# Recurrent-branch projection units computed with tokens in partitions, scaled by ScalarE, turned by VectorE in 32x32 blocks; convolution taps placed later

## The chip, the cores and the metric

The kernel runs on 1 core of one Trainium2 chip. The metric is the device time of one launch in microseconds (us). Weights come from HBM; activations, split weights and intermediate slabs stay in SBUF, and matmul sums are built in PSUM.

## The reference, cut to what matters

Two transformer-like blocks are computed in float32 for 256 tokens of width 2048. The change touches the first part of the first one:

```
h    = rmsnorm(x, norm_mix_pre)
proj = h @ w_in                       # columns: xr 2048, yr 2048, q 2048, k 256, v 256, gates 4096
xr   = causal_depthwise_conv(xr, conv_w, conv_b)    # y[t] = b + sum_k x[t-3+k] * w[k], 4 taps
xr   = rg_lru(xr, ...)                # gates by small matmuls, then a scan over tokens
y_rnn = xr * gelu(yr)
q, k = rope(q), rope(k)
y_att = sliding_window_sink_attention(q, k, v, attn_sinks)
mix  = sigmoid(g_rnn) * (y_rnn @ w_rnn_proj) + sigmoid(g_attn) * (y_att @ w_attn_proj)
```

The norm's factor of each token (`rstd`) is not in `h` as the kernel holds it: it is multiplied in when a projection is copied out of PSUM.

## The kernel before

Every large product is cut into **units** of 512 output columns and all 2048 rows of the weight: 16 k-tiles of 128 rows. Two k-tiles are one **step**, so a unit has 8. The inputs and weights are split into a high and a low part (`h_hi`, `h_lo`, `w_hi`, `w_lo`), and three products are added: high by high, high by low, low by high. For each step SyncE loads 512 KB into `raw`, ScalarE writes `w_hi` (`split_hi`, line 670), VectorE writes `w_lo` as `raw - w_hi` (`split_lo`, line 1185, instruction at 1187), and TensorE runs the matmuls (`unit`, line 1954). `raw`, `w_hi` and `w_lo` are rings of 4, so the split of step j+3 may begin once TensorE is done with step j-1.

A unit comes in two forms. **With tokens in partitions** the activations are the stationary operand and 512 weight columns are streamed: 16 k-tiles x 2 token tiles x 3 products = 96 matmuls of 512 columns (lines 1995 to 1997). **By feature** (`by_feature=True`) the weights are stationary and 256 tokens are streamed: 16 x 4 x 3 = 192 matmuls of 256 columns (lines 1987 to 1990), and the output has features in partitions.

The part that matters is a sequence of units on TensorE: k/v, q0, xr0, q1, xr1, q2, xr2, q3, xr3, then yr0 to yr3. I call the pair xr(c), q(c+1) **round** c (for c = 3 the pair is xr3, yr0). Beside round c runs the attention of 8 heads for q(c), cut in four parts p of two heads, placed by hand at k-tiles or steps:

- `rotate_q` (line 1382), VectorE, at the start of round c: four instructions for each of two token tiles. Lines 1349 and 1350 read `acc` in PSUM and one SBUF table. Lines 1352 and 1353 read `tmp` and `tmp2`, both in SBUF, and write `stg`.
- `turn` (line 2003), TensorE, after the 4th k-tile of xr(c): it waits for `stg_ready`, which `rotate_q` gives, and transposes `stg` into `tps`. `q_copy` (line 764), ScalarE, copies it to `q_c`.
- `scores` (2079, TensorE), `soft` (1395, VectorE), `exps` (771, ScalarE), `totals` (1406, VectorE), `normalise` (520, GpSimd), `turn_p` (2091, TensorE), `pt_copy` (784, ScalarE), `by_v` (2101, TensorE), `y_hi` (788, ScalarE), `y_lo` (1412, VectorE), in this order for each part. `y_hi` and `pt_copy` of part 3 stand in the last two steps of the round.

The recurrent branch in round c: `xr_out` (1423), VectorE, in the first step after xr(c), copies `acc[0]` to `xr_c` and multiplies it by a row of the tokens' factors. `conv_taps` (794), ScalarE, writes the four scaled taps, each of 4 instructions: k = 3 into `slab_d`, k = 2, 1, 0 into `taps`, in steps 0, 2, 5 and 5 of the second unit. `conv_sum` (530), GpSimd, adds k = 2, 1, 0 into `slab_d` in place, one instruction each, each waiting for its tap; both inputs are in SBUF. GpSimd's program is a strict sequence: four `normalise`, then three `conv_sum`, for each round. Later `gates` (831, ScalarE) waits for the last sum and for `rg` (2126, TensorE), which computes the gate products.

The order of each engine's work is written out: `steps` runs a split and then the hooks of that step. `placed` sorts hooks by step; within a step they run in the order in which they were listed. ScalarE and VectorE run rounds 0 to 2 as a hardware loop and round 3 as straight code.

Of the kernel before, what the change touches and what calls it, by code (L numbers as in the profile page):

```python
# [16 lines left out]
P = 128  # L17
# [3 lines left out]
ALU = mybir.AluOpType  # L21
# [5 lines left out]
TT = SEQ // P  # L27
# [68 lines left out]
def griffin_block_then_ssm_block(nc, a, inv_freq, out):  # L96
    with ExitStack() as ctx:
# [81 lines left out]
        part_hi, part_lo = sem("part_hi"), sem("part_lo")  # L179

# [453 lines left out]
        TAPS_AT = [8, 10, 13, 13]  # L634
# [27 lines left out]
        def _(act):  # L662
# [100 lines left out]
            def attention(i, c):  # L763
# [29 lines left out]

                def conv_taps(k):

                    if k == 3:
                        act.wait_ge(acc_free[0], lin(i, 1, c + 2))
                        act.wait_ge(conv_ready, lin(i, 1, c + 1))
# [21 lines left out]
            with act.Fori(0, NH - 1) as i:  # L820
                beside_xr, beside_q = attention(i, 0)
                steps(i, 2 * S, (U_QX + 1) * S, beside_xr)
                steps(i, 2 * S, (U_QX + 2) * S, beside_q)
            beside_xr, beside_yr = attention(None, NH - 1)
            steps(None, 0, (U_QX + 2 * NH - 1) * S, beside_xr)

# [354 lines left out]
        def _(dve):  # L1181
# [18 lines left out]

            def turning(i, stride, index):


                def two(n):
                    if n == 0:
                        dve.wait_ge(sum_ready, lin(i, stride, index + 1))
                    for q in (2 * n, 2 * n + 1):
                        a, b = divmod(q, 4)
                        src = tmp[32 * a:32 * a + 32, :, :].rearrange("p t (m q i) -> p t m q i", q=4, i=32)[:, :, :, b, :]
                        dst = turned4[32 * b:32 * b + 32, :, :].rearrange("p m (t q i) -> p t m q i", t=TT, q=4)[:, :, :, a, :]  # L1210
                        ins = V.transpose(dst, src)  # L1211
                    if n == 7:
                        ins.then_inc(blocks_turned, 1)
# [168 lines left out]
            def rotate_q(i, c):  # L1382

                unit_over(i, 2 * S, (U_QX + 2 * c) * S)
                if i is None:
                    dve.wait_ge(tps_ready, T_K + 1)
# [7 lines left out]
            def attention(i, c):  # L1394
# [22 lines left out]

                places = []
                for p, at in enumerate(SOFT_AT):
                    places += [(at, lambda p=p: soft(p)), (at + 2, lambda p=p: totals(p)), (Y_ATT_AT[p], lambda p=p: y_lo(p))]  # L1420
                return placed(places, S, 2)[0]
# [10 lines left out]
            with dve.Fori(0, NH - 1) as i:  # L1432
                with chain.loop(i, NH - 1, 19):
                    beside_xr, beside_q = attention(i, 0)
                    steps(i, 2 * S, (U_QX + 1) * S, beside_xr)
                    beside_q[0] = [lambda: xr_out(i, 0)] + beside_q.get(0, [])
                    steps(i, 2 * S, (U_QX + 2) * S, beside_q)
                    rotate_q(i, 1)
            beside_xr, beside_yr = attention(None, NH - 1)
            steps(None, 0, (U_QX + 2 * NH - 1) * S, beside_xr)  # L1440
            beside_yr[0] = [lambda: xr_out(None, NH - 1)] + beside_yr.get(0, [])
# [42 lines left out]
            for c in range(NH):  # L1484
# [4 lines left out]
                unit_over(None, 0, u * S)  # L1489
# [863 lines left out]
```

## Time and profile before

| | |
|---|---|
| median of 3 runs | 2240.53 us (2240.46 to 2240.60) |
| the profiled execution's own time | 2240.62 us |
| its span, first to last instruction | 2238.9 us |
| VectorE busy | 1575.0 us, 70% |
| ScalarE busy | 1218.3 us, 54% |
| GpSimd busy | 275.1 us, 12% |
[...]

The profile's page gives the busy time of each engine, the chain of work that ended last and the costliest groups of instructions. A matmul's record is longer than the distance to the next one, since matmuls are pipelined: what a stream of them takes is read from the distance between two starts, not from the durations. In the timeline a row is start, duration, engine, line, operation, output and inputs, shape, count, and in brackets the idle time before it with what ended it.

### The profile page before, as it was taken

What the parts mean: (1) busy time and instruction counts of PE and PEld (TensorE: products, weight loads), DVE (VectorE), ACT (ScalarE), POOL (GpSimd) and SP (SyncE); (2) the same over time, 40 slices, a digit from 0 to 9 for tenths busy, and PEclk for the clock granted to TensorE, in tenths of its full rate; (3) what the DMA queues carried; (4) which work ended last, traced back from release to release, by engine and by line L of the source; (5) the groups of instructions that cost most, each with busy time, mean ns of one, the idle gap of its engine ahead of it and who ended that gap; (6) DMA issues with size and microseconds to landing.
All of it is one profiled execution on the core that took longest, in us unless ns stands there. A gap on an engine that the chain in (4) does not pass through costs nothing.

```text
span 2238.9 us, 32782 instructions
## 1 busy us (share of the span) xinstructions
PE 2227.7 (99%) x11645; PEld 1875.1 (84%) x11645; DVE 1575.0 (70%) x2081; ACT 1218.3 (54%) x1915; POOL 275.1 (12%) x319
## 2 busy tenths in 40 slices
PE   9999999999999999999999999999999999999999
PEld 7888999888888888888888888889987788888887
DVE  6666657664664778757857856966999967766774
ACT  6666667544444456555655656555444446554443
POOL 2132220000000102211212121120000001110000
PEclk9999999999999999999999999999999999999999
DMA  8555454666666856666666666665666655555665
GB/s 242 153 170 150 144 186 142 191 194 194 193 189 197 255 189 213 206 208 190 219 206 193 215 209 204 192 219 177 185 185 206 194 179 168 168 161 177 199 200 167
DMA packets 215350, 427.09 MB, mean 191 GB/s; under 512 B 14097, under 2 KB 14385, under 8 KB 214961
## 3 DMA queue, kind: packets, MB, share of 16 engines
q1 hardware_dynamic: 206960, 398.57, 57.3%
q0 software_dynamic: 8048, 26.62, 3.9%
q8 instruction: 91, 1.49, 0.3%
q14 instruction: 43, 0.34, 0.0%
q10 hardware_dynamic: 208, 0.07, 0.0%
HBM read 414.71 MB, written 10.49 MB: 190 GB/s over the span
## 4 chain that ended last, share of the span: by engine, by line
PE 93%; DVE 3%; ACT 2%; issue 1%; DMA 0%; POOL 0%; DVEq 0%; ACTq 0%
PE acc L1995 26%; PE acc L1997 26%; PE acc L1996 26%; PE acc L1987 4%; PE acc L1989 3%; PE acc L1990 3%; PE sides L2213 1%; PE tps L2223 1%; PE sides L2087 1%; PE tps L2105 1%; DVE w_lo L1187 1%; ACT w_hi L674 1%; PE tps L2098 0%; ACT tmp L851 0%; DVE tmp L1466 0%
## 5 line engine op out<-in xcount | busy, mean ns | idle before, releaser
L1187 DVE TENSOR_TENSOR w_lo<-raw,w_hi 128x1024 fp32r<-128x1024 f32 x752 | 927.4, 1243 | 574.1 <-ACT w_hi L674 568.7
L674 ACT ACTIVATE w_hi<-raw 128x1024 fp32r<-128x1024 f32 x752 | 790.3, 1058 | 729.1 <-PE acc L1997 598.1
L1995 PE MATMUL acc<-w_hi,h_hi 128*128 128x512 f32 x1440 | 569.5, 395 | 2.7 <-DVE w_lo L1187 1.8
L1997 PE MATMUL acc<-w_hi,h_lo 128*128 128x512 f32 x1440 | 561.1, 390 | 0.0
L1996 PE MATMUL acc<-w_lo,h_hi 128*128 128x512 f32 x1440 | 560.7, 389 | 0.0
L1995 PEld LDWEIGHTS acc<-w_hi,h_hi 128*128 128x128 f32 x1440 | 270.4, 188 | 69.4 <-issue 15.1
L1997 PEld LDWEIGHTS acc<-w_hi,h_lo 128*128 128x128 f32 x1440 | 270.3, 188 | 57.2
L1996 PEld LDWEIGHTS acc<-w_lo,h_hi 128*128 128x128 f32 x1440 | 270.6, 188 | 53.3
L1995 PE MATMUL acc<-w_hi,slab_dg_r 128*128 128x512 f32 x756 | 294.1, 389 | 0.0
L1996 PE MATMUL acc<-w_lo,slab_dg_r 128*128 128x512 f32 x756 | 294.1, 389 | 0.0
L1997 PE MATMUL acc<-w_hi,slab_dg_r 128*128 128x512 f32 x756 | 294.1, 389 | 0.0
L1987 PE MATMUL acc<-h_hi,w_hi 128*128 128x256 f32 x768 | 221.3, 288 | 0.8 <-issue 0.8
L1989 PE MATMUL acc<-h_lo,w_hi 128*128 128x256 f32 x768 | 217.2, 283 | 0.0
L1990 PE MATMUL acc<-h_hi,w_lo 128*128 128x256 f32 x768 | 217.1, 283 | 0.0
L1211 DVE STREAM_TRANSPOSE stg<-tmp 32x256 f32<-32x256 f32 x384 | 167.3, 436 | 5.8
L1997 PEld LDWEIGHTS acc<-w_hi,slab_dg_r 128*128 128x128 f32 x756 | 141.9, 188 | 29.5
L1996 PEld LDWEIGHTS acc<-w_lo,slab_dg_r 128*128 128x128 f32 x756 | 141.9, 188 | 29.4
L1995 PEld LDWEIGHTS acc<-w_hi,slab_dg_r 128*128 128x128 f32 x756 | 141.9, 188 | 29.4
L1987 PEld LDWEIGHTS acc<-h_hi,w_hi 128*128 128x128 f32 x768 | 146.8, 191 | 7.1 <-issue 6.9
L1989 PEld LDWEIGHTS acc<-h_lo,w_hi 128*128 128x128 f32 x768 | 147.0, 191 | 0.2
L1990 PEld LDWEIGHTS acc<-h_hi,w_lo 128*128 128x128 f32 x768 | 146.9, 191 | 0.0
L1995 PE MATMUL acc<-w_hi,slab_f_r 128*128 128x512 f32 x256 | 100.4, 392 | 0.0
(390 smaller groups left out, 2320.4 us busy)
## 6 DMA issues: line engine op xcount, KB each, us to landing
raw<-in_w_in_dram SPq DMA_DIRECT2D x328, 512.0 KB, 4.0
raw<-in_w_mlp_up_dram SPq DMA_DIRECT2D x128, 512.0 KB, 4.2
raw<-in_w_mlp_down_dram SPq DMA_DIRECT2D x128, 512.0 KB, 4.4
raw<-in_w_out_dram SPq DMA_DIRECT2D x64, 512.0 KB, 4.4
raw<-in_w_rnn_proj_dram SPq DMA_DIRECT2D x32, 512.0 KB, 4.0
raw<-in_w_attn_proj_dram SPq DMA_DIRECT2D x32, 512.0 KB, 4.1
trig_scratch<-tmp POOLq DMA_DIRECT2D x32, 256.0 KB, 4.8
raw<-in_w_proj_ssm_dram SPq DMA_DIRECT2D x16, 512.0 KB, 3.8
```

Of the source, the lines that this page charges most:

```text
L674: nc.scalar.activation(w_hi[:, j % RING], raw[:, j % RING], ACT.Copy).then_inc(hi_ready, 1)
L1187: V.tensor_tensor(w_lo[:, j % RING], raw[:, j % RING], w_hi[:, j % RING].bitcast(F32), ALU.subtract)\
L1211: ins = V.transpose(dst, src)
L1987: T.matmul(o, wh[:, c], hi[:, k, :], start=first and m % 2 == 0, stop=False, skip_group_check=True)
L1989: T.matmul(o, wh[:, c], lo[:, k, :], start=False, stop=False, skip_group_check=True)
L1990: ins = T.matmul(o, wl[:, c], hi[:, k, :], start=False, stop=last, skip_group_check=True)
L1995: T.matmul(o, hi[:, k, c], wh, start=first, stop=False)
L1996: T.matmul(o, hi[:, k, c], wl, start=False, stop=False)
L1997: ins = T.matmul(o, lo[:, k, c], wh, start=False, stop=last)
L2087: ins = T.matmul(side[n][:, t * P:t * P + (t + 1) * P], q_c[at, p, t * P:(t + 1) * P], k_c[at, 0:(t + 1) * P], start=True, stop=True)
L2105: ins = T.matmul(y_banks[64 * n:64 * n + 64, t, :], v_c[:, s, :], prob_t[p % 2][:, n, b * P:(b + 1) * P], start=s == 0, stop=s == t)
L2213: ins = T.matmul(side[j % 2][:, part * SEQ:(part + 1) * SEQ], b_t[at, part, :], u_feat[at, n // 4, :], start=True, stop=True)
```

## The change

The four xr units drop `by_feature`: they are computed with tokens in partitions. What copies them out changes with that.

- ScalarE: a new `xr_stage`, first hook of the step after xr(c), copies the two token tiles of `acc[0]` to `tmp` with `rstd` as scale (2 instructions of 128x512) and frees the bank.
- VectorE: `xr_out` is gone. A new `xr_turn` turns `tmp` into `xr_c` by 16 transposes of 32x256 elements in 32x32 blocks, two to a hook, in steps 0, 1, 1, 1, 3, 3, 4, 5 of the second unit.
- `conv_taps` wait for the last transpose (`xr_turned`). k = 3 moves to step 6 and k = 2 to step 7 of the second unit; k = 1 and k = 0 move to steps 0 and 1 of the next xr unit, ahead of the other hooks there. In round 3 all of k = 2, 1, 0 are in step 7.
- The loops of ScalarE and VectorE over rounds 0 to 2 are written out.

```diff
-        TAPS_AT = [8, 10, 13, 13]
+        TAPS_AT = [14, 15]
+        XR_TURN_AT = [0, 1, 1, 1, 3, 3, 4, 5]
...
+                def xr_stage():
+
+                    unit_over(None, 0, (U_QX + 1 + 2 * c) * S)
+                    act.wait_ge(stg_ready, T_QX + c + 1)
+                    for t in range(TT):
+                        ins = nc.scalar.activation(tmp[:, t, :], tok(acc[0])[:, t, :], ACT.Copy, scale=rstd[:, t:t + 1])
+                    ins.then_inc(acc_free[0], 1)
...
                     if k == 3:
-                        act.wait_ge(acc_free[0], lin(i, 1, c + 2))
-                        act.wait_ge(conv_ready, lin(i, 1, c + 1))
+                        act.wait_ge(xr_turned, c + 1)
+                        act.wait_ge(conv_ready, c + 1)
...
-                places = [(2, q_copy)]
+                places = [(2, q_copy), (S, xr_stage)]
...
-                places += [(at, lambda k=k: conv_taps(k)) for at, k in zip(TAPS_AT, (3, 2, 1, 0))]
-                return placed(places, S, 2)[0]
+                late = [lambda: conv_taps(1), lambda: conv_taps(0)]
+                places += [(at, lambda k=k: conv_taps(k)) for at, k in zip(TAPS_AT, (3, 2))]
+                if c == NH - 1:
+                    places += [(TAPS_AT[-1], f) for f in late]
+                return placed(places, S, 2)[0] + [late]
...
+            for c in range(NH):
+                beside_xr, beside_yr, next_late = attention(None, c)
+                for at, f in enumerate(late):
+                    beside_xr[at] = [f] + beside_xr.get(at, [])
+                late = next_late
...
+            def turn_two(n, to):
+
+                for q in (2 * n, 2 * n + 1):
+                    a, b = divmod(q, 4)
+                    src = tmp[32 * a:32 * a + 32, :, :].rearrange("p t (m q i) -> p t m q i", q=4, i=32)[:, :, :, b, :]
+                    dst = to[32 * b:32 * b + 32, :, :].rearrange("p m (t q i) -> p t m q i", t=TT, q=4)[:, :, :, a, :]
+                    ins = V.transpose(dst, src)
+                return ins
...
+                def xr_turn(n):
+                    if n == 0:
+                        dve.wait_ge(acc_free[0], c + 2)
+                        if c:
+                            dve.wait_ge(tap_ready, 4 * c)
+                    ins = turn_two(n, xr_c)
+                    if n == 7:
+                        ins.then_inc(xr_turned, 1)
...
-            def xr_out(i, c):
-                unit_over(i, 2 * S, (U_QX + 1 + 2 * c) * S)
-                rows_ = row[:, :].unsqueeze(1).broadcast_to([P, QPC, SEQ])
-                dve.wait_ge(row_copied, 1)
-                dve.wait_ge(conv_ready, lin(i, 1, c + 1))
-                V.tensor_tensor(xr_c, feat(acc[0]), rows_, ALU.mult).then_inc(acc_free[0], 1)
...
-                unit(None, 0, u * S, 0, u, h_hi, h_lo, by_feature=True, hooks=beside_xr)
+                unit(None, 0, u * S, 0, u, h_hi, h_lo, hooks=beside_xr)
```

## Rows read from the trace of the kernel before

**Rows 1.** The page: busy time, share of the span and instructions of each engine
```profile
PE 2227.7 (99%) x11645; PEld 1875.1 (84%) x11645; DVE 1575.0 (70%) x2081; ACT 1218.3 (54%) x1915; POOL 275.1 (12%) x319
```
**Rows 2.** Window sums, round 2: PE, PEld, DVE, ACT, POOL busy, clock, DMA
```profile
172.00:228.60 56.60, 56.60 (x401) 48.90 (x401) 36.23 (x53) 37.40 (x83) 16.36 (x12) 1.00 0.50 149
```
**Rows 3.** Waits of TensorE from 100 us on, the longest: total, times, longest
```profile
PE tps L2278 <- DVE tmp L1859: 0.9, 1, 0.9
```
**Rows 4.** Timeline, TensorE: twelve 512-column matmuls, then nine of 256, then the turn
```profile
56.23 0.39 PE L1995 MATMUL acc<-w_hi,h_hi 128*128 128x512 f32 x1
...
58.95 0.28 PE L1987 MATMUL acc<-h_hi,w_hi 128*128 128x256 f32 x1
...
176.74 0.28 PE L1987 MATMUL acc<-h_hi,w_hi 128*128 128x256 f32 x1
...
177.82 1.04 PE L2010 MATMUL tps<-ident,stg 128*128 128x128 f32 x8
```
**Rows 5.** Timeline, TensorE: first matmuls of q3, of xr3, of yr0, of yr1
```profile
200.43 0.50 PE L1995 MATMUL acc<-w_hi,h_hi 128*128 128x512 f32 x1
...
228.61 0.28 PE L1987 MATMUL acc<-h_hi,w_hi 128*128 128x256 f32 x1
...
256.98 0.38 PE L1987 MATMUL acc<-h_hi,w_hi 128*128 128x256 f32 x1
...
286.03 0.28 PE L1987 MATMUL acc<-h_hi,w_hi 128*128 128x256 f32 x1
```
**Rows 6.** Each line's own view: instructions, duration in ns min/median/max, first and last start
```profile
L894 ACT ACTIVATE tmp<-acc,small x16: 680/685/690, 412.8 to 710.5; 128x512 f32<-128x512 f32 x16
L1211 DVE STREAM_TRANSPOSE stg<-tmp x384: 425/436/445, 474.2 to 2161.6; 32x256 f32<-32x256 f32 x192
L803 ACT ACTIVATE slab_dg_f<-slab_dg_f,pt x16: 585/587/606, 89.6 to 260.5; 128x256 f32 x12, 128x256 f32<-128x256 f32 x4
```
**Rows 7.** Timeline, VectorE: a split in step 4 of q2
```profile
160.54 1.23 DVE L1187 TENSOR_TENSOR w_lo<-raw,w_hi 128x1024 fp32r<-128x1024 f32 x1 [2.06 <-ACT w_hi L674]
```
**Rows 8.** Timeline, ScalarE, end of q2: taps k = 1, pt_copy, y_hi
```profile
162.53 1.69 ACT L806 ACTIVATE slab_e_f<-slab_dg_f,pt 128x254 f32<-128x254 f32 x4
...
167.13 0.82 ACT L786 ACTIVATE slab_e_f<-tps 128x768 f32<-128x768 f32 x1 [0.36 <-PE tps L2098]
...
170.77 0.39 ACT L791 ACTIVATE slab_f_r<-tps 128x256 f32 x1 [1.20 <-PE tps L2105]
```
**Rows 9.** Timeline, VectorE, start of round 2: rotate_q's first, third and last instruction
```profile
172.26 0.69 DVE L1349 TENSOR_TENSOR tmp<-acc,cosb 128x512 f32<-128x512 f32 x1 [0.45 <-PE acc L1997]
...
173.58 0.42 DVE L1352 TENSOR_TENSOR stg<-tmp 128x256 f32<-128x256 f32 x1
...
175.92 0.42 DVE L1353 TENSOR_TENSOR stg<-tmp 128x256 f32<-128x256 f32 x1
```
**Rows 10.** Timeline, GpSimd: the last sum of round 1; two sums of round 3
```profile
170.47 3.26 POOL L534 TENSOR_TENSOR slab_dg_f<-slab_dg_f,slab_i_f 128x1012 f32<-128x1012 f32 x1
...
280.07 2.38 POOL L534 TENSOR_TENSOR slab_dg_f<-slab_dg_f,slab_e_f 128x1016 f32<-128x1016 f32 x1
...
282.53 3.21 POOL L534 TENSOR_TENSOR slab_dg_f<-slab_dg_f,slab_i_f 128x1012 f32<-128x1012 f32 x1
```
**Rows 11.** Timeline, VectorE, the same stretches: splits beside those sums, and a y_lo
```profile
169.60 1.87 DVE L1187 TENSOR_TENSOR w_lo<-raw,w_hi 128x1024 fp32r<-128x1024 f32 x1 [1.45 <-ACT w_hi L674]
171.40 0.41 DVE L1416 TENSOR_TENSOR slab_h_r<-tps,slab_f_r 128x256 f32 x1
...
280.52 3.00 DVE L1187 TENSOR_TENSOR w_lo<-raw,w_hi 128x1024 fp32r<-128x1024 f32 x1 [2.46 <-ACT w_hi L674]
283.52 3.30 DVE L1187 TENSOR_TENSOR w_lo<-raw,w_hi 128x1024 fp32r<-128x1024 f32 x1
```
**Rows 12.** Timelines, ScalarE and TensorE: pt_copy of part 0 and by_v behind it, xr1
```profile
140.29 0.79 ACT L786 ACTIVATE slab_e_f<-tps 128x768 f32<-128x768 f32 x1
...
142.22 0.33 PE L2105 MATMUL tps<-slab_e_f,pi 128*64 128x128 f32 x2
```

More of the change, by code:

```diff
@@ L179, in griffin_block_then_ssm_block @@
         part_hi, part_lo = sem("part_hi"), sem("part_lo")
+        xr_turned = sem("xr_turned")
         side_landed = sem("side_landed")
@@ L819, in _ @@
             steps(None, 0, U_QX * S, {3: [lambda: row_copy(1)], 4: [exponentials], 5: [k_copy]})
[L820 to L825, printed above, removed]
+            late = []
+            for c in range(NH):
[3 more added lines that the diff above has]
+                late = next_late
+                steps(None, 0, (U_QX + 1 + 2 * c) * S, beside_xr)
+                if c < NH - 1:
+                    steps(None, 0, (U_QX + 2 + 2 * c) * S, beside_yr)
             def y_high(c):
@@ L1206, in two @@
                         dve.wait_ge(sum_ready, lin(i, stride, index + 1))
[L1207 to L1211, printed above, removed]
+                    ins = turn_two(n, turned4)
                     if n == 7:
@@ L1384, in rotate_q @@
                 unit_over(i, 2 * S, (U_QX + 2 * c) * S)
-                if i is None:
+                if c == 0:
                     dve.wait_ge(tps_ready, T_K + 1)
@@ L1420, in attention @@
                     places += [(at, lambda p=p: soft(p)), (at + 2, lambda p=p: totals(p)), (Y_ATT_AT[p], lambda p=p: y_lo(p))]
+                places += [(S + at, lambda n=n: xr_turn(n)) for n, at in enumerate(XR_TURN_AT)]
                 return placed(places, S, 2)[0]
-            def xr_out(i, c):
-                unit_over(i, 2 * S, (U_QX + 1 + 2 * c) * S)
-                rows_ = row[:, :].unsqueeze(1).broadcast_to([P, QPC, SEQ])
-                dve.wait_ge(row_copied, 1)
-                dve.wait_ge(conv_ready, lin(i, 1, c + 1))
-                V.tensor_tensor(xr_c, feat(acc[0]), rows_, ALU.mult).then_inc(acc_free[0], 1)
             steps(None, 0, U_QX * S, {3: [lambdas], 5: [softplus]})
             rotate_q(None, 0)
[L1432 to L1441, printed above, removed]
+            for c in range(NH):
+                beside_xr, beside_yr = attention(None, c)
+                steps(None, 0, (U_QX + 1 + 2 * c) * S, beside_xr)
+                if c < NH - 1:
+                    steps(None, 0, (U_QX + 2 + 2 * c) * S, beside_yr)
+                    rotate_q(None, c + 1)
             no_reset = keep[:, 0:1, :].broadcast_to([P, QPC, SEQ])
@@ L1489, in _ @@
                 unit_over(None, 0, u * S)
+                if c == 0:
+                    dve.wait_ge(row_copied, 1)
                 rows_ = row[:, :].unsqueeze(1).broadcast_to([P, QPC, SEQ])
@@ L2120, in _ @@
                 u = U_QX + 1 + 2 * c
-                unit(None, 0, u * S, 0, u, h_hi, h_lo, by_feature=True, hooks=beside_xr)
+                unit(None, 0, u * S, 0, u, h_hi, h_lo, hooks=beside_xr)
                 unit(None, 0, (u + 1) * S, 0, u + 1, h_hi, h_lo, hooks=beside_q)
             beside_xr, beside_yr = attention(None, NH - 1)
-            unit(None, 0, (U_QX + 2 * NH - 1) * S, 0, U_QX + 2 * NH - 1, h_hi, h_lo, by_feature=True, hooks=beside_xr)
+            unit(None, 0, (U_QX + 2 * NH - 1) * S, 0, U_QX + 2 * NH - 1, h_hi, h_lo, hooks=beside_xr)
             def rg(c):
```

## The prediction, made before the result was known

> **What bounds the kernel now.** I read the page's busy line first: TensorE is busy for 2227.7 of 2238.9 us, VectorE for 70%, ScalarE for 54%, GpSimd for 12% [rows 1]. [...] The view of waits lists nothing for TensorE inside the changed rounds, and from 100 us to the end its longest is 0.9 us, far later [rows 3]. So two things alone can move the time: the length of TensorE's own stream, and a wait that TensorE does not have today. Work added to VectorE or ScalarE costs nothing until something that TensorE waits for comes late.
>
> **TensorE's stream.** Twelve 512-column matmuls take 58.95 - 56.23 = 2.72 us, 226.7 ns each; nine of 256 columns take 177.82 - 176.74 = 1.08 us, 120 ns each [rows 4]. A unit by feature is 192 x 120 = 23.04 us, one with tokens in partitions 96 x 226.7 = 21.76 us: 1.28 us less. The hooks between the matmuls take some of that back. The pair q3 and yr0 shows it, since both carry the same seven hooks: q3 takes 228.61 - 200.43 = 28.18 us with tokens in partitions, yr0 takes 286.03 - 256.98 = 29.05 us by feature [rows 5]. That is 0.87 us, so 0.41 us is lost at seven hooks, 0.06 at each. An xr unit has four hooks, or five with the one behind its last matmul but one step: 1.28 - 4 x 0.06 = 1.04, I take 1.05 us a unit, **4.2 us for four**. Bounds: 4 x 0.87 = 3.5 and 4 x 1.28 = 5.1.
>
> By these rows one matmul costs its columns and 13.3 ns, since 2 x 120 - 226.7 = 13.3. [...]
>
> **What is added, and what hides it.** *ScalarE*: two copies of 128x512 for each of four rounds; a line of that shape from the same bank takes 0.685 us [rows 6], 1.4 us a round in step 0 of the second unit, where ScalarE waited for xr_out before. Its reader, y_hi of part 0, comes 1.2 us later than today, but VectorE reads that result only after what was xr_out, so nothing behind it moves. *VectorE*: 16 transposes of 0.436 us, with no overlap from one to the next 0.45 us [rows 6], 7.2 us a round, less the 1.2 us of xr_out. By step: 0.9, 2.7, 0, 1.8, 0.9, 0.9 us in steps 0 to 5. The split after step 3 began at 160.54 after 2.06 us of idle time [rows 7], which takes in the 1.8; in the other steps a split may come late by most of a step of 2.7 us, since the ring holds three steps. VectorE's load in a round rises from 36 to 42 of 55.5 us. By this I cost it at nothing; if the cover were gone it would be at most the excess over those gaps, a few tenths of a us in a round. The unrolled loops are cost at nothing: round 3 was straight code before and kept TensorE as full as the others. *The shorter xr unit* leaves the softmax chain less time. pt_copy of part 0 ends at 141.08, and by_v, which waits for it, starts at 142.22 [rows 12]: 1.1 us in hand, of which the shorter unit takes 0.6. It holds, by half a us.
>
> **The taps, and GpSimd behind them.** This is where I expect the loss. Today the four taps are done before step 6, so the three sums run over steps 5 to 8, and the last one ends at 170.47 + 3.26 = 173.73, just as rotate_q reads two SBUF tiles for the first time, at 173.58 and for 0.42 us [rows 9, 10]. In the changed order I follow ScalarE at the end of q2 in the durations of today [rows 6, 8]. pt_copy ends at 167.95 at the earliest, as TensorE sets it. Taps k = 3 are four instructions of 0.52 us: to 169.9. The split of step 7: to 170.85. y_hi is released at 170.77: to 171.15. Taps k = 2, 1.6 us (1.69 with the last one's end): to 172.75. The split of step 0 of xr2: to 173.7. Taps k = 1: to 175.3. The split of step 1: to 176.2. Taps k = 0: to 177.9. GpSimd's sums start behind k = 2, 1, 0: at about **172.9, 175.4 and 178.0**, each 2.38 us long where nothing disturbs it [rows 10]. They now lie exactly beside rotate_q of the next round, 172.4 to 176.4.
>
> What a sum does to VectorE is in the rows. A split, two SBUF inputs, takes 1.23 us alone [rows 7]. Beside the sums it took 3.00 us from 280.52 and 3.30 us from 283.52 [rows 11]. The first ended at 283.52, 1.07 us behind the sum that ended at 282.45; the second at 286.82, 1.08 us behind the sum that ended at 285.74 [rows 10, 11]. So it did not run slower, it stood until the sum was over. In return the sum that came while a split was waiting took 3.21 or 3.26 us and not 2.38. y_lo, one input in PSUM, took its 0.41 us beside a running sum [rows 11]. [...]
>
> In rotate_q lines 1352 and 1353 have two SBUF inputs, four instructions in all; 1349 and 1350 read PSUM and are free. Placed against the three sums: line 1349 starts at 172.4, 1350 at 173.0, 1352 is ready at 173.7 and stands until the first sum ends at 175.3. Then either 1353 or the second sum goes first, 30 ns apart. If the sum: 1353 ends at 178.1, 1349 and 1350 bring the next 1352 to 179.3, inside the third sum, which ends at 180.4, and 1353 ends at 180.95. If 1353: the second sum is pushed to 178.1, the next 1352 stands until then, the third sum goes ahead of the last 1353 and ends at 180.6, and 1353 ends at 180.9. Both orders give **180.9**, where today it is 176.34 [rows 9].
>
> Who waits: TensorE's turn. It stands behind four k-tiles, due 24 x 0.2267 us behind the first matmul of xr2, which today comes 48 x 0.12 before the turn's 177.82, at 172.06 [rows 4]: at 177.5. It would start at 181.0: **3.45 us of wait in each of rounds 1, 2 and 3**, 10.3 us. Behind the waiting turn on TensorE is the whole rest of the stream, so this is a full loss; q_copy, the splits and scores move with the turn, and their distance to it stays as it was. In round 0 there are no sums yet and no wait. In round 3's second unit no rotation follows; the sums run to about 295, splits beside them stand for up to 2.4 us, but TensorE has 6.9 us of gate products to do there and three steps in the ring. Bounds of the wait: 0, if VectorE and GpSimd do not exclude each other for these instructions; 1.3 us, if both instructions of a pair pass between two sums (1353 then ends near 178.7); and 4 us with the sums a few tenths later or longer.
>
> **The sum.** Against the profiled execution's own 2240.62 (span 2238.9, 1.7 outside it), 0.09 above the median of the runs: 2240.62 - 4.2 + 10.3 = 2246.7, so **2246.6 us** on the median's scale, +0.27%. Its own range: waits of 3.0 to 4.0 with gains of 3.5 to 5.1 give 2244.4 to 2249.0.
>
> **The rivals.**
> *No wait at the turn.* If rotate_q's pairs pass beside the sums, or the sums come too late to meet them, only the gain is left: 2240.5 - 4.2 = 2236.3, between 2235.4 and 2237.0. For it speaks that no row of before shows one of these 256-element instructions beside a running sum; against it, that a split of the same form stands in both cases in which it meets one. It decides at 1.1 us of delay: rotate_q ends at 176.4 undisturbed, the turn is due at 177.5.
> *Half a wait.* 1.3 us a round: 2240.5 - 4.2 + 3.9 = 2240.2. For it: the second and third sum start only 0.1 to 0.3 us before the point at which a pair would pass.
> [...]
> [...]
>
> **How the numbers follow.** Full wait 0.50, no wait 0.24, half a wait 0.15, no shorter stream 0.03, more than the turn 0.08. A measurement of this kernel can tell about 0.2%, or 4.5 us, from no change: 2236.05 and 2245.0. Faster by more needs no wait and a gain over 4.5 of the possible 3.5 to 5.1, about half of that case: 0.13. Slower: the full wait but for its lowest end, and the last case: 0.55. Within: 0.32. The range goes from 2236.2, which takes in half of the no-wait case, to 2249.5.
>
> **What would show it.** In the profile after: matmuls of xr units 226.7 ns apart and round 0 shorter by about 1.05 us; three waits of TensorE at line 2010's counterpart for the last line of rotate_q, near 3.4 us each; lines 1352 and 1353 with durations of 1 to 3 us in rounds 1 to 3 and 0.42 in round 0; sums of GpSimd that start 0.8, 3.3 and 5.9 us behind the first matmul of xr1, xr2, xr3; transposes at 0.44 us. I am wrong if those lines keep 0.42 us beside a sum, if the sums start later than 1.7 us behind that matmul, or if TensorE waits elsewhere, first of all at by_v of part 0.

## The result

The changed kernel takes 2250.38 us (median of 5 runs, 2249.33 to 2254.87) against 2240.53 (5 runs, 2240.23 to 2240.60). The ratio is 1.005, with a 95% interval of 1.0039 to 1.0061: it is slower by half a per cent. The forecast was 2246.6 with a range up to 2249.5, so the direction was right and the time lies 0.9 us above the range. Of the 27 runs of the kernel before that stand beside three of the experiments below, one took 4522.61 us, twice the others; the ratios leave it out.

In the kernel after, `split_lo` is line 1203, the rotation's four lines are 1370, 1371, 1373 and 1374 (for 1349, 1350, 1352 and 1353), the turn is line 2032 (for 2010), `scores` 2109, the sums 535, the splits to `w_hi` 676, and matmuls by tokens are 2017 to 2019. The page's busy line of the kernel after, beside [rows 1]:

```profile
PE 2227.7 (99%) x11261; PEld 1854.6 (82%) x11261; DVE 1607.5 (71%) x2141; ACT 1223.0 (54%) x1923; POOL 267.6 (12%) x319
```

TensorE's busy time is what it was, 2227.7, and that is the first thing to be puzzled by: the units have become shorter. The view of waits of TensorE between 40 and 320 us, kernel after, where before had nothing (engine, output, line, what it waited for: us in total, times, the longest):

```profile
PE tps L2032 <- DVE stg L1374: 9.5, 3, 3.2
```

Three waits of 3.2 us at the turn, for the last line of `rotate_q`: the place and the number that the prediction names. TensorE's timeline of the kernel before, the turn of round 0, and of the kernel after, the turns of rounds 0 to 3 and the first scores behind two of them (a count below 8 is that of a view cut at its window's edge):

```profile
64.71 1.04 PE L2010 MATMUL tps<-ident,stg 128*128 128x128 f32 x8
```
```profile
63.90 1.09 PE L2032 MATMUL tps<-ident,stg 128*128 128x128 f32 x8
...
122.74 1.97 PE L2032 MATMUL tps<-ident,stg 128*128 128x128 f32 x8 [3.17 <-DVE stg L1374]
127.96 0.93 PE L2109 MATMUL sides<-k_c,slab_dg_f 64*128 64x128 f32 x8
...
183.08 1.27 PE L2032 MATMUL tps<-ident,stg 128*128 128x128 f32 x8 [3.19 <-DVE stg L1374]
188.45 0.92 PE L2109 MATMUL sides<-k_c,slab_dg_f 64*128 64x128 f32 x7
...
243.52 0.66 PE L2032 MATMUL tps<-ident,stg 128*128 128x128 f32 x4 [3.17 <-DVE stg L1374]
```

The balance is made with window sums from the turn of round 0 to the turn of round 3, and from the first matmul of yr0 to the end. Columns as in [rows 2]. Before:

```profile
64.71:234.37 169.66, 169.66 (x1203) 146.63 (x1202) 109.62 (x161) 112.23 (x249) 51.81 (x37) 1.00 0.53 156
256.98:2238.90 1981.92, 1974.64 (x9942) 1655.90 (x9940) 1405.96 (x1788) 1053.11 (x1566) 208.16 (x250) 1.00 0.62 193
```

After:

```profile
63.90:243.52 179.62, 170.09 (x912) 132.44 (x912) 137.66 (x204) 116.62 (x256) 44.64 (x37) 0.98 0.49 147
265.42:2248.70 1983.28, 1975.31 (x9942) 1655.41 (x9940) 1409.61 (x1803) 1053.51 (x1569) 207.90 (x251) 1.00 0.63 193
```

| stretch | before | after | difference |
|---|---|---|---|
| start to the turn of round 0 | 64.71 | 63.90 | -0.81 |
| three rounds, turn to turn | 169.66 | 179.62 | +9.96 |
| turn of round 3 to yr0 | 22.61 | 21.90 | -0.71 |
| yr0 to the end | 1981.92 | 1983.28 | +1.36 |
| span | 2238.9 | 2248.7 | +9.8 |

Of the three rounds' 179.62 us TensorE stood for 9.53. The other 170.09 are still 0.43 more than before, although the same 912 instructions take 166.42 us in a run below that has no wait (`psum_rot`). So 3.67 us of work time were added: the mean clock of the stretch is 0.98, and the next view shows where. Window sums of the kernel after around the three turns:

```profile
119.20:122.70 3.50, 0.36 (x2) 0.00 (x0) 3.48 (x2) 1.52 (x3) 3.42 (x3) 0.96 0.00 0
122.70:124.40 1.70, 1.66 (x9) 1.67 (x9) 1.57 (x2) 0.00 (x0) 1.70 (x3) 0.50 0.20 36
124.40:126.00 1.60, 1.60 (x6) 1.31 (x5) 1.60 (x2) 1.26 (x3) 0.88 (x2) 0.55 0.98 312
126.00:131.00 5.00, 5.00 (x27) 3.64 (x26) 2.10 (x3) 1.33 (x2) 0.00 (x0) 1.00 0.91 328
...
184.80:186.40 1.60, 1.60 (x5) 1.22 (x5) 1.60 (x2) 1.11 (x2) 0.00 (x0) 0.50 0.46 55
...
243.50:245.20 1.70, 1.68 (x12) 1.55 (x13) 1.58 (x2) 0.55 (x3) 0.00 (x0) 1.00 0.00 0
```

Behind the wait of round 1 the granted clock is 0.50 for about 3 us; a like stretch lies behind that of round 2; in round 3 it stays at 1.00. From the turn to the first scores it takes 127.96 - 122.74 = 5.22 us in round 1 and 188.45 - 183.08 = 5.37 in round 2, where round 0 (to 67.67) and round 3 (to 247.29) have 3.77: 3.05 us of the 3.67. The other 0.6, 0.2 for each wait, lies at the edges of the waits: from the turn of round 0 to that of round 1 it is 122.74 - 63.90 = 58.84, less 166.42 / 3 = 55.47, so a wait that is recorded as 3.17 us costs 3.37. Of the -0.81 ahead of the turn of round 0, 0.77 is there before the first changed unit begins, at 58.18 for 58.95 [rows 4], so no changed unit makes it. `form_only` below, whose program up to that matmul is that of the kernel before, begins xr0 at 57.98, and all ten other profiles lie between 57.78 and 58.46: it is the profile of before that stands apart, and why stays open. Of the rest of the run more below. All together: three rounds' gain -3.24 (`psum_rot` has it alone), xr3's end -0.71, round 0 -0.04, waits 3 x 3.37 = +10.1, clock +3.05, start -0.77, rest +1.36, which is 9.8. TensorE's busy time is unchanged because the shorter units (-4.0) are nearly made up for by matmuls at the lower clock (+3.05) and by what lies outside the changed rounds (+0.6).

Where the 3.2 us come from, VectorE's timeline of the kernel after at the start of round 1, and GpSimd's beside it:

```profile
115.56 1.79 DVE L1373 TENSOR_TENSOR stg<-tmp 128x256 f32<-128x256 f32 x1
117.27 0.41 DVE L1374 TENSOR_TENSOR stg<-tmp 128x256 f32<-128x256 f32 x1
...
118.92 1.30 DVE L1373 TENSOR_TENSOR stg<-tmp 128x256 f32<-128x256 f32 x1
120.14 2.54 DVE L1374 TENSOR_TENSOR stg<-tmp 128x256 f32<-128x256 f32 x1
```
```profile
114.67 2.39 POOL L535 TENSOR_TENSOR slab_dg_f<-slab_dg_f,slab_e_f 128x1020 f32<-128x1020 f32 x1 [9.48 <-ACT slab_e_f L816]
117.28 2.65 POOL L535 TENSOR_TENSOR slab_dg_f<-slab_dg_f,slab_e_f 128x1016 f32<-128x1016 f32 x1 [0.22 <-ACT slab_e_f L816]
120.02 2.38 POOL L535 TENSOR_TENSOR slab_dg_f<-slab_dg_f,slab_i_f 128x1012 f32<-128x1012 f32 x1
```

The instructions that take 0.42 us alone [rows 9] take 1.79, 0.41, 1.30 and 2.54. The first stands until the first sum ends at 117.06 and runs 0.29 us beyond it; the second passes between two sums; the third stands for the second sum; the last one stands for the whole third sum and ends 0.28 us behind it, at 122.68, and TensorE's turn starts at 122.74.

### The profile page after: what moved, and what is told of

Same layout as the page of the kernel before. It is cut to its first block, busy times and chain, and to the rows that moved or that the text cites. A ratio compares the mean times of both kernels' runs of the same rounds, so it can differ in the third digit from the quotient of the medians.

```text
span 2248.7 us, 31819 instructions
## 1 busy us (share of the span) xinstructions
PE 2227.7 (99%) x11261; PEld 1854.6 (82%) x11261; DVE 1607.5 (71%) x2141; ACT 1223.0 (54%) x1923; POOL 267.6 (12%) x319
## 4 chain that ended last, share of the span: by engine, by line
PE 89%; DVE 6%; ACT 3%; issue 1%; DMA 1%; POOL 0%; DVEq 0%; ACTq 0%; SPq 0%; POOLq 0%
PE acc L2017 26%; PE acc L2019 25%; PE acc L2018 25%; PE acc L2009 2%; PE acc L2011 2%; PE acc L2012 2%; DVE w_lo L1203 1%; ACT w_hi L676 1%; PE sides L2235 1%; PE tps L2245 1%; PE sides L2109 1%; DVE stg L1373 0%; DMA raw<-in_w_out_dram 0%; PE tps L2120 0%; PE tps L2127 0%
## 5 line engine op out<-in xcount | busy, mean ns | idle before, releaser
L2017 PE MATMUL acc<-w_hi,h_hi 128*128 128x512 f32 x1568 | 622.2, 397 | 1.9 <-DVE w_lo L1203 1.0
L2019 PE MATMUL acc<-w_hi,h_lo 128*128 128x512 f32 x1568 | 611.9, 390 | 0.0
L2018 PE MATMUL acc<-w_lo,h_hi 128*128 128x512 f32 x1568 | 611.4, 390 | 0.0
L2017 PEld LDWEIGHTS acc<-w_hi,h_hi 128*128 128x128 f32 x1568 | 295.1, 188 | 76.0 <-issue 16.9
L2009 PE MATMUL acc<-h_hi,w_hi 128*128 128x256 f32 x512 | 147.4, 288 | 0.8 <-issue 0.8
L2011 PE MATMUL acc<-h_lo,w_hi 128*128 128x256 f32 x512 | 144.8, 283 | 0.0
L2012 PE MATMUL acc<-h_hi,w_lo 128*128 128x256 f32 x512 | 144.8, 283 | 0.0
L2009 PEld LDWEIGHTS acc<-h_hi,w_hi 128*128 128x128 f32 x512 | 98.0, 191 | 4.3 <-issue 4.2
L2019 PE MATMUL acc<-w_hi,slab_h_r 128*128 128x512 f32 x256 | 99.7, 389 | 0.0
L2018 PE MATMUL acc<-w_lo,slab_f_r 128*128 128x512 f32 x256 | 99.6, 389 | 0.0
```

Source lines behind the costliest of these rows:

```text
L2009: T.matmul(o, wh[:, c], hi[:, k, :], start=first and m % 2 == 0, stop=False, skip_group_check=True)
L2011: T.matmul(o, wh[:, c], lo[:, k, :], start=False, stop=False, skip_group_check=True)
L2012: ins = T.matmul(o, wl[:, c], hi[:, k, :], start=False, stop=last, skip_group_check=True)
L2017: T.matmul(o, hi[:, k, c], wh, start=first, stop=False)
L2018: T.matmul(o, hi[:, k, c], wl, start=False, stop=False)
L2019: ins = T.matmul(o, lo[:, k, c], wh, start=False, stop=last)
```

## The experiments

The runs were made on other chips of the same type. The kernel before took 2240.60 us (26 runs), 2240.65 (27 runs) and 2240.32 (1 run) there. The table has all of them; the ratio is to the kernel before on the same chip. `small_sums` leaves out most of the convolution's additions, and `form_only` and `form_unrolled` still copy the xr block out as if it were by feature, so that the recurrent branch's values land in the wrong places.

| run | what it is | us, median (range) | ratio, 95% interval |
|---|---|---|---|
| psum_rot | after, `rotate_q`'s second product in PSUM | 2236.33 (2235.46 to 2237.08) | 0.998 (0.9971 to 0.9989) |
| small_sums | after, sums of one token column each | 2236.45 (2235.88 to 2237.38) | 0.998 (0.9971 to 0.999) |
| form_unrolled | before, xr by tokens, loops written out | 2236.92 (2236.32 to 2237.95) | 0.9983 (0.9974 to 0.9992) |
| form_only | before, xr by tokens | 2237.98 (2236.99 to 2238.76) | 0.9989 (0.998 to 0.9998) |
| sums_behind | after, sums behind `rotate_q` | 2245.32 (2244.54 to 2246.75) | 1.0021 (1.0011 to 1.003) |
| filled | after, TensorE kept at work before the turn | 2246.21 (2245.92 to 2246.69) | 1.0026 (1.0016 to 1.0035) |
| taps_late | after, xr by feature, no transposes | 2253.94 (2252.82 to 2254.43) | 1.0061 (1.0046 to 1.0076) |
| again_a, again_b | after, unchanged | 2250.42; 2255.78 | one run each |

### psum_rot: is it the second SBUF input?

```diff
-                xs = tmp2[:, t, 0:heads * 64].rearrange("p (h u f) -> p h u f", u=2, f=32)
+                xs = second[:, t, 0:heads * 64].rearrange("p (h u f) -> p h u f", u=2, f=32)
...
-                                 t == TT - 1)
+                                 t == TT - 1, tok(sides) if c else tmp2)
```

> The changed kernel with one thing different: in rounds 1 to 3 rotate_q writes its second product into the PSUM tile `sides` in place of `tmp2`, so the two combining instructions read one SBUF tile and one PSUM tile. Theory (GpSimd's sums hold off VectorE instructions with two SBUF inputs): the combining instructions take 0.4 to 0.5 us beside a sum, rotate_q ends within 1.1 us of its old time, TensorE's three waits at the turn (3.2 us each) and the low clock behind them vanish: 2236 to 2238 us. Rival (VectorE simply has too much to do with 16 more transposes a round): the waits stay, 2250 us. A third outcome: the splits behind rotate_q still stand beside the second and third sum and make the softmax of part 0 late; then TensorE waits at by_v for up to 1 us a round, 2237 to 2240.

It is. The waits of TensorE between 40 and 320 us, then VectorE's timeline in round 1, then GpSimd's, all of this run:

```profile
PE tps L2032 <- DVE stg L1374: 0.7, 1, 0.7
```
```profile
115.94 0.42 DVE L1373 TENSOR_TENSOR stg<-tmp,sides 128x256 f32<-128x256 f32 x1
116.28 0.41 DVE L1374 TENSOR_TENSOR stg<-tmp,sides 128x256 f32<-128x256 f32 x1
...
118.83 2.31 DVE L1203 TENSOR_TENSOR w_lo<-raw,w_hi 128x1024 fp32r<-128x1024 f32 x1
...
121.06 3.39 DVE L1203 TENSOR_TENSOR w_lo<-raw,w_hi 128x1024 fp32r<-128x1024 f32 x1
```
```profile
115.05 2.41 POOL L535 TENSOR_TENSOR slab_dg_f<-slab_dg_f,slab_e_f 128x1020 f32<-128x1020 f32 x1 [9.46 <-ACT slab_e_f L816]
```

A sum runs from 115.05 to 117.46, and lines 1373 and 1374 take 0.42 and 0.41 us in the middle of it, with one input in PSUM. The one wait left is that of round 0, 0.7 us, where there is no sum. The splits behind the rotation still stand beside the later sums, 2.31 and 3.39 us for 1.23, and nobody waits for them: here the ring of three steps is the cover. The same three rounds and the rest, window sums of this run:

```profile
64.27:230.69 166.42, 166.42 (x912) 130.39 (x913) 132.59 (x205) 114.74 (x255) 42.78 (x36) 1.00 0.53 159
252.53:2234.60 1982.07, 1974.79 (x9942) 1657.26 (x9940) 1411.19 (x1803) 1053.99 (x1569) 207.38 (x251) 1.00 0.62 193
```

169.66 - 166.42 = 3.24 us in three rounds, 1.08 for each xr unit. And the rest behind yr0 is 1982.07, where the kernel after had 1983.28 with the same program; `small_sums` has 1982.98 there (span 2234.7, yr0 at 251.72), `filled` 1982.25, `form_only` 1983.32, `again_b` 1983.03. It varies by 1.2 us among kernels that do the same in it, and 1981.92 of before lies just beside that, so of the 1.36 us in the balance nothing can be put down to the change. The three profiles of the kernel after agree within 0.25 us there, so it is not mere chance from run to run; its cause stays open.

The spans of before and of this run differ by 4.3 us, 2238.9 and 2234.6. Of that, 0.95 us lies ahead of the first changed unit (58.00 for 58.95). The changed units themselves give 3.24 us in the three rounds and 0.77 from the turn of round 3 to yr0 (21.84 for 22.61), less 0.51 for the wait in round 0: 3.5 us.

### small_sums: is it the length of the sums?

```diff
-                        o = slab_d[:, c * QPC:(c + 1) * QPC, 3 - k:]
-                        ins = pool.tensor_tensor(o, o, taps[k][:, :, 3 - k:], ALU.add)
+                        o = slab_d[:, c * QPC:(c + 1) * QPC, 3 - k:4 - k]
+                        ins = pool.tensor_tensor(o, o, taps[k][:, :, 3 - k:4 - k], ALU.add)
```

> The kernel after, but each of GpSimd's three sums a round adds one token column of every feature instead of all of them (most of the convolution's additions are left out); waits, places and everything else as they were. My theory: the length of these sums beside rotate_q is the whole loss, so each sum takes a few tenths of a us, no instruction of rotate_q takes more than 0.8 us, TensorE stands at no turn of rounds 1 to 3, the clock stays at 1.00, and the time is that of the version that keeps rotate_q out of their way by PSUM, 2236 to 2237 us. The rival that ScalarE's late taps or VectorE's transposes themselves make rotate_q late: the waits of 3.2 us stay, 2249 to 2251 us.

VectorE's timeline of this run in round 1, and GpSimd's:

```profile
115.12 0.42 DVE L1373 TENSOR_TENSOR stg<-tmp 128x256 f32<-128x256 f32 x1
...
117.46 0.42 DVE L1374 TENSOR_TENSOR stg<-tmp 128x256 f32<-128x256 f32 x1
```
```profile
114.24 0.21 POOL L535 TENSOR_TENSOR slab_dg_f<-slab_dg_f,slab_e_f 128x4 f32<-128x4 f32 x1 [9.47 <-ACT slab_e_f L816]
```

`rotate_q` writes its products to SBUF again, GpSimd waits for the taps as before, the late taps of ScalarE and the 16 transposes of VectorE are all there, and the lines of `rotate_q` take 0.42 us. (The third sum, behind `rotate_q`, takes 1.06 us beside a split that was there first, more than the few tenths expected; nobody waits for it.) TensorE has no wait between 40 and 320 us, and the time is that of `psum_rot`. Two ways of ending the overlap, by the operand and by the length, give the same 2236.4: the blocking, with what follows its waits, is the whole loss, and the transposes and the copies by ScalarE cost nothing that can be measured.

### taps_late: does the place of the taps do it alone?

```diff
-                places = [(2, q_copy), (S, xr_stage)]
+                places = [(2, q_copy)]
...
-                places += [(S + at, lambda n=n: xr_turn(n)) for n, at in enumerate(XR_TURN_AT)]
-                return placed(places, S, 2)[0]
+                return placed([(S, xr_out)] + places, S, 2)[0]
...
-                unit(None, 0, u * S, 0, u, h_hi, h_lo, hooks=beside_xr)
+                unit(None, 0, u * S, 0, u, h_hi, h_lo, by_feature=True, hooks=beside_xr)
```

> One part of the change alone: the convolution taps at their new places and the loops written out, but xr units by feature and the old copy out of PSUM, so no transposes and no staging copies. Theory (the place of the sums is the cause): rotate_q ends as late as in the changed kernel, the turn is due 0.32 us later, so it waits 2.9 us in each of rounds 1 to 3, with 0 to 5 us in all of low clock behind it: 2249 to 2254 us. Rival (the transposes' load on VectorE is the cause): no wait, 2240.5 us.

Its waits of TensorE between 40 and 320 us, and the last line of `rotate_q` in round 2:

```profile
PE tps L2031 <- DVE stg L1374: 8.7, 3, 2.9
```
```profile
181.83 2.55 DVE L1374 TENSOR_TENSOR stg<-tmp 128x256 f32<-128x256 f32 x1
```

Three waits of 2.9 us, 0.3 less than in the kernel after, since the turn is due 5.76 us behind the first matmul of a unit by feature and 5.44 us behind that of one with tokens in partitions. The time is above that of the kernel after by 3.6 us: it has the loss and not the gain. So the later taps alone bring the waits (the loops are written out here too, but that alone brings no such wait, as `form_unrolled` shows below).

### form_only and form_unrolled: what is the shorter unit worth?

```diff
-                unit(None, 0, u * S, 0, u, h_hi, h_lo, by_feature=True, hooks=beside_xr)
+                unit(None, 0, u * S, 0, u, h_hi, h_lo, hooks=beside_xr)
```

> The other part alone: the kernel before with only the form of the four xr units changed to tokens in partitions; taps, copies and loops as before. The result is not the reference's, since the copy out takes the block as if it were by feature. [...] If the shorter xr unit makes the softmax chain or the turn late, the time lies between 2236.3 and 2240 with waits of TensorE at the turn of q0 or at by_v.

By the rows of before the stream gains 1.05 us a unit, which is 2236.3 us without a wait. The time of 2237.98 us is that of the case with waits, between 2236.3 and 2240. Its waits of TensorE between 40 and 320 us, and the one at by_v in round 1:

```profile
PE tps L2105 <- ACT slab_e_f L786: 1.2, 3, 0.4
PE tps L2010 <- DVE stg L1353: 0.4, 1, 0.4
```
```profile
159.60 0.88 PE L2105 MATMUL tps<-slab_e_f,pi 128*64 128x128 f32 x12 [0.41 <-ACT slab_e_f L786]
```

Three waits of 0.4 us at by_v, at 103.67, 159.60 and 215.55, one in each looped round and none in round 3. They are not at part 0, as the expectation of `form_unrolled` below has it. In round 1 the four by_v start at 140.14, 150.61, 159.60 and 168.16, so the one that waits is that of part 2, in the second unit of the round. At part 0 the pt_copy ends at 139.53 and by_v starts at 140.14 without a wait: the half us of the prediction is there, 0.6 us. Part 2 had nothing in hand already in the kernel before, in ScalarE's and TensorE's timeline of round 1:

```profile
160.41 0.79 ACT L786 ACTIVATE slab_e_f<-tps 128x768 f32<-128x768 f32 x1
...
161.25 0.88 PE L2105 MATMUL tps<-slab_e_f,pi 128*64 128x128 f32 x12
```

The copy ends at 161.20, 0.05 us ahead of by_v. `form_unrolled` is `form_only` with the loops over rounds written out, ScalarE's as shown and VectorE's in the same way:

```diff
-            with act.Fori(0, NH - 1) as i:
-                beside_xr, beside_q = attention(i, 0)
-                steps(i, 2 * S, (U_QX + 1) * S, beside_xr)
-                steps(i, 2 * S, (U_QX + 2) * S, beside_q)
+            for c in range(NH - 1):
+                beside_xr, beside_q = attention(None, c)
+                steps(None, 0, (U_QX + 1 + 2 * c) * S, beside_xr)
+                steps(None, 0, (U_QX + 2 + 2 * c) * S, beside_q)
```

> The kernel before with the xr units by tokens in partitions and nothing else of the change, as in the run form_only (the copy-out is that of before, so the recurrent branch's values land in the wrong places), but with ScalarE's and VectorE's loops over rounds 0 to 2 written out. The run with the loops had waits of 0.4 us at by_v of part 0 in each looped round, 1.2 us in all, that the changed kernel, written out, does not show. If the loop's own instructions use up the half us in hand at by_v, these waits are gone here: 2236.6 to 2237.3 us, about 1 us under the run with the loops. If it is the load on ScalarE (taps ahead of the softmax chain, as before) and not the loop, the waits stay at 0.4 us a round and the time at 2238.0.

```profile
PE tps L2009 <- DVE stg L1353: 0.8, 2, 0.5
PE acc L1994 <- DVE w_lo L1187: 0.2, 1, 0.2
```

The waits at by_v are gone, two of up to 0.5 us stand at the turns of rounds 0 and 3, and the time is 1.06 us lower, 2236.92. In the profiles the stretch from the first matmul of xr0 to that of yr0 falls from 195.70 to 194.93 us, by 0.77. So the loops' own instructions on ScalarE or VectorE (these runs do not part the two) made ScalarE's copy late, and writing them out is not free of effect, as I had costed it, but worth 0.8 to 1 us once the units are shorter. The time is 0.6 us above `psum_rot`, too little to put down to anything.

### sums_behind: would another place for the sums do?

```diff
                         pool.wait_ge(tap_ready, 4 * c + 4 - k)
+                        if k == 2 and c < NH - 1:
+                            pool.wait_ge(stg_ready, T_QX + c + 2)
```

> The kernel after, but in rounds 0 to 2 the first sum of GpSimd also waits until rotate_q of the next round is done, so that the sums run behind it. Theory A, which follows the blocking further: rotate_q ends about 4.3 us behind the first matmul of the unit and the turn has no wait; the three sums then run from 4.3 to about 13 us behind that matmul, each time one split, softmax step or total of VectorE stands for up to 2.4 us, and the chain to by_v of part 0, with about half a us in hand, comes late: waits of TensorE at scores, turn_p or by_v of 1 to 4 us a round, 2240 to 2250 us. Theory B, only rotate_q has no slack: no wait anywhere, 2236 to 2238 us.

Its waits of TensorE between 40 and 320 us, and GpSimd's last sum and a split of VectorE beside the sums in round 1:

```profile
PE tps L2122 <- POOL slab_i_f L526: 3.4, 3, 1.1
PE sides L2111 <- DVE slab_i_f L1420: 2.6, 3, 0.9
PE tps L2129 <- ACT slab_e_f L790: 2.1, 3, 0.7
```
```profile
124.60 3.24 POOL L537 TENSOR_TENSOR slab_dg_f<-slab_dg_f,slab_i_f 128x1012 f32<-128x1012 f32 x1
```
```profile
118.88 3.41 DVE L1205 TENSOR_TENSOR w_lo<-raw,w_hi 128x1024 fp32r<-128x1024 f32 x1
```

The turn is free, and 8.1 us of waits stand one stage further down: at `turn_p` (2122) for `normalise`, at `scores` (2111) for `soft`, at by_v (2129) for `pt_copy`. 2236.4 + 8.1 = 2244.5, measured 2245.32. Theory A holds; a split that stands for 3.4 us hurts nobody in `psum_rot`, but when the sums of round 1 start 4.5, 8.1 and 11.4 us behind the first matmul of xr1 (113.23), for 0.7, 3.3 and 5.9 in `psum_rot`, the softmax chain behind the splits is late. No wait of this run reaches 1.2 us, and its clock stays at 1.00.

### filled, again_a and again_b: what do the waits cost beside themselves?

```diff
-                places = [(3, lambda: turn(i, 1, T_QX + c))]
+                def turn_q():
+                    if c:
+                        pe.wait_ge(sc_read, 4 * c)
+                        keep_turning(26)
+                    turn(i, 1, T_QX + c)
+
+                places = [(3, turn_q)]
```

> The changed kernel with 26 small transposes of the identity on TensorE ahead of the turn in rounds 1 to 3, about 2.8 us of work that only fills the wait. Theory (the low clock behind the waits is set off by TensorE's standing still, and makes up 3.2 us of the profiled time and the spread of the runs): the granted clock stays at 1.00, the filler and what is left of the wait add up to the same 3.2 us, the time falls by 3 to 4 us to 2246 to 2247.5 and the runs agree within 0.5 us. Rival (the clock falls for another reason or costs nothing): the time stays at 2250 with the same spread, or rises by what the filler adds.

`filled` has TensorE turn an identity matrix 26 times in the time in which it would stand. Its waits of TensorE, and the turn of round 1 with the first scores behind it:

```profile
PE tps L2032 <- DVE stg L1374: 1.1, 3, 0.4
```
```profile
122.70 1.09 PE L2032 MATMUL tps<-ident,stg 128*128 128x128 f32 x8 [0.38 <-DVE stg L1374]
126.47 0.93 PE L2109 MATMUL sides<-k_c,slab_dg_f 64*128 64x128 f32 x8
```

The turn is as late as in the kernel after, 122.70 for 122.74, but the scores come 3.77 us behind it and not 5.22. The granted clock is 1.00. The median falls by 4.2 us to 2246.21, and the spread from 5.5 us to 0.8, a little more than the 0.5 expected. So what follows the waits, and the spread, comes from TensorE's standing still.

The kernel after was profiled twice more. In its first profile the granted clock was 0.50 behind two of the three waits, rounds 1 and 2, and it took 1.45 and 1.60 us longer from the turn to the first scores than behind the third.

> The kernel after, unchanged, profiled once more. [...] My theory, that this comes and goes from turn to turn and run to run and makes the spread of its times: waits of 3.2 us three times again, and a time of 2247.2 us plus about 1.5 us for each turn with a low clock behind it, so 2247.2, 2248.8, 2250.3 or 2252.0. The rival, that the waits themselves differ from run to run and the clock is a bystander: waits of 3.2 us that change with the time.

> The same kernel as again_a, for a third profile, with the same expectations: three waits of 3.2 us whatever the time, and the time by the number and length of the stretches at the lower clock.

The waits of TensorE of again_a, then of again_b, and around the turn of round 1 of again_b the window sums:

```profile
PE tps L2032 <- DVE stg L1374: 9.6, 3, 3.2
```
```profile
PE tps L2032 <- DVE stg L1374: 10.4, 4, 3.2
```
```profile
123.50:125.20 1.70, 1.68 (x9) 1.68 (x9) 1.59 (x2) 0.00 (x0) 1.70 (x3) 0.50 0.38 63
125.20:127.00 1.80, 1.80 (x7) 1.42 (x6) 1.80 (x2) 1.47 (x3) 0.86 (x2) 0.50 0.95 305
127.00:129.00 2.00, 2.00 (x6) 1.62 (x5) 0.11 (x1) 0.05 (x1) 0.00 (x0) 0.50 0.93 329
129.00:131.00 2.00, 2.00 (x13) 1.18 (x13) 0.00 (x0) 0.84 (x1) 0.00 (x0) 0.92 0.97 346
```

The three waits are 3.2 us again in both (the fourth of again_b is 0.8 us in round 0). again_a has a granted clock of 0.50 behind rounds 1 and 3 and 1.00 behind round 2, and its 2250.42 is one of the times expected. again_b has 0.50 behind all three, and each time for 5.6 to 5.8 us from the start of the turn: 6.4 to 6.5 us from turn to scores, 2.7 more than without, 8.0 in all. Its 2255.78 is above everything that I had listed, since I took 1.5 us as the price of one. So in three profiles the waits are constant and the clock makes the difference; the five timed runs of the result fit that, with mean clocks of 0.998, 0.998, 0.997, 0.997 and 0.995 at 2250.38, 2249.33, 2250.26, 2253.78 and 2254.87 us. The price of one wait beside its own length is 0, about 1.5 or 2.7 us, and what decides between them these runs don't show.

## Why the prediction was right in direction and 3.8 us short

| step of the prediction | forecast | measured |
|---|---|---|
| gain of an xr unit | 1.05 | 1.08 (psum_rot, three rounds) |
| matmuls of xr units apart | 226.7 ns | 226.7 ns |
| sums start behind the first matmul of xr1 (113.94) | 0.8, 3.3, 5.9 | 0.7, 3.3, 6.1 |
| `rotate_q` of round 1 ends later by | 4.6 | 4.4 (from 114.24 to 122.68, 8.44 us; 4.06 in psum_rot) |
| wait of the turn, rounds 1, 2, 3 | 3.45 each | 3.2 recorded, 3.37 in cost |
| transposes and their place | free, 0.44 us each | free, 0.436 us |
| ScalarE's copies | free | free |
| wait in round 0 | none | 0.3, none and 0.8 in the three profiles |
| slack of by_v, part 0 | holds by half a us | holds, by 0.6 us in `form_only` |
| slack of by_v, part 2 | not in the prediction | 0.05 us in before; short by 0.4 us a round in `form_only` |
| loops written out | free | 0.8 to 1 us gained (`form_only` to `form_unrolled`) |
| clock behind the waits | unchanged (chance of a fall 0.08) | 0.50 behind two or three of the three waits |

**What held.** The whole mechanism: GpSimd's sums land on `rotate_q`, exclude its instructions with two SBUF inputs, push the turn, and TensorE, which has no slack, stands for it: 1.3 to 2.5 us for 0.42, and waits of 3.2 us. Even the order, line 1374 ahead of the second sum, is the second of the two that the prediction follows. Without the clock the sum is confirmed to 0.4 us: 2246.6 forecast, 2246.21 in `filled`, where the turn is as late and the clock stays up. That it fits so closely is in part luck. Between the profiles of before and of `filled`, 0.53 us is gained ahead of xr0 and 0.33 us lost behind the start of yr0, and the prediction has neither. Of its own terms in the kernel after, the gain was 4.0 us for 4.2 and the waits 10.1 for 10.3, and these two misses cancel.

**The term that was mis-sized** is the clock. The prediction gives 0.08 to "more than the turn", the case that the granted clock falls behind the waits. I had taken the price as that of one step at half the clock for each wait, 12 x 226.7 ns = 2.7 us once more, 8 us for three, and a time of 2254.7; that the clock would fall at all was my estimate. The forecast itself takes it as zero and lets the range end at 2249.5. It was not a rival: it came in every profile of the kernel after, in two or three of three places, and in `taps_late` too. Its price of 2.7 us for one, a step at half speed, was the right upper end, as again_b shows. Measured is 3.05 us in all in the first profile, 3.2 in again_a and 8.0 in again_b, where the forecast's sum has nothing. A forecast with half of it, as the runs have it at the median, would have been 2246.6 + 4 = 2250.6. The argument for 0.08 was only that no row of before shows a fall, but before has no wait longer than 0.9 us from 100 us on [rows 3], so it could show none: absence of the case is no evidence on it, and its bound belonged in the range.

**Smaller things that were not seen.** In round 0 the turn is due 5.44 us behind the first matmul of xr0 and no longer 5.76, and `rotate_q` ends 5.24 us behind it in before, 5.66, 5.15 and 6.38 in the three profiles of the kernel after: the wait is 0.3 us, none, and 0.8, and differs from run to run of one kernel. I had looked for waits in the rounds with sums only. At by_v the prediction has part 0 only, and names it as the first place for a wait. Its slack was read rightly; the place without slack was part 2, where the copy ended 0.05 us ahead already in before, and there `form_only` waits 0.4 us in each looped round. In the kernel after, written out, nothing waits there. The other rivals fell: rows of these 256-element instructions beside a sum now exist and show 1.3 to 2.5 us, all but the one that starts together with the second sum ("no wait"); the second instruction of the first pair does pass between two sums, but the second pair meets both of the others ("half a wait"); and the stream is shorter by 1.08 us a unit. The 0.03 for "no shorter stream" was an estimate with a smaller gain, which no run shows: 3.24 us were measured for three units.

**What beats both.** `psum_rot` computes the same outputs in 2236.33 us, 4.3 us under the kernel before, of which the profiles put 3.5 down to the changed units: the change's gain is real, and the 14 us between `psum_rot` and the kernel after are what the place of the taps costs, with the low clock behind the waits in it. It needs only that one of the products of `rotate_q` is written to a PSUM tile that is free at that time.

## What to carry to other kernels

When work is moved, list what its consumers on GpSimd will now run beside, and look there for VectorE instructions with two SBUF inputs that somebody waits for; one operand in PSUM took them out of it here, 0.42 us beside a sum for up to 2.55. Moving the GpSimd work a few us further is no cure where a chain without slack follows: it moved 9.5 us of waits to 8.1 us elsewhere. And a forecast wait of TensorE of some 3 us carries a second price, matmuls at a granted clock of 0.50 behind it (seven of nine waits of 3.2 us here, 1.5 to 2.7 us each), which belongs in the sum with its bounds even if the kernel before has no such wait to read it from.

## What the runs showed of the hardware

**The clock falls behind a wait of 3 us, and not every time.** In the three profiles of the kernel after, nine waits of 3.2 us were followed seven times by matmuls at a granted clock of 0.50, for 3.1 to 5.8 us behind the start of the turn, 1.5 to 2.7 us lost each time, and twice by none. Behind two of the three waits of 2.9 us in `taps_late` the granted clock was 0.50 too (125.0 to 127.0 and 186.0 to 188.0) and it took 5.4 us from turn to scores; behind the third it was 1.00 and took 3.9. No wait of 1.1 us or less had it (psum_rot, sums_behind, filled); between 1.1 and 2.9 us there is none in these rounds. TensorE had been busy for 50 of 50 us at a granted clock of 1.00 before each, and `filled`, with work in the same place, has no fall, so it is the stand itself that matters; its length alone does not decide. One of the 27 runs of the kernel before, of which no trace was kept, has a mean granted clock of 0.949 and 2244.22 us, 3.6 above the median, so that a lower clock without these waits can't be excluded.

**How VectorE and GpSimd take turns.** An instruction of 256 elements beside a sum took 0.42 us in `psum_rot`, with `sides` in PSUM, and 2.54 in the kernel after, with both inputs in SBUF beside a sum of 2.38. With a queue on both sides the rows show this. An instruction of 256 elements that stood ran on 0.28 us beyond the end of the sum. At the second sum of rounds 1 to 3 of the kernel after, instruction and sum are recorded within 0.01 us of each other, at 117.27 and 117.28, 177.61 and 177.60, 238.06 and 238.06; VectorE's went first each time, and the sum then took 2.65 to 2.67 us for 2.38. The recorded order does not tell which: in round 2 of `sums_behind`, with the sum at 176.20 and a split at 176.21, the split stood and took 3.45 us. One recorded 0.12 us behind a sum's start, at 120.14 for 120.02, stood for all of it and took 2.54. Four instructions of 0.42 us, 1.7 us of work, thus took 6.0 us against three sums of 7.4 us.
